# Expert biases as fp32 rows on partitions 96 to 127, and a 22nd early chunk in the long convolution's buffer

## The chip, the core and the metric

The kernel runs on one NeuronCore of a Trainium2 chip. The metric is the device time of one execution in microseconds, as the median of several runs. The profile is one execution recorded by the hardware profiler. Engines are named as in its rows: PE (TensorE matmuls), PEld (its weight loads), DVE (VectorE), ACT (ScalarE), POOL (GpSimd), SP (SyncE, whose queue issues nearly all loads of weights; SPq in the rows).

## What is computed

One step of a one-layer decoder on 264 tokens (256 of a prompt and 8 samples), all in fp32 with a model width of 1024. In short:

```python
proj = rmsnorm(x) @ w_in                      # 7184 columns: q, k, v, z, beta, a, glu, gates
branch_a = gated_delta_net(q, k, v, ...) @ w_gdn_out
branch_b = silu(layernorm(long_conv(glu))) @ w_conf_out     # 31 taps
x = x + (g_a * branch_a + g_b * branch_b) @ w_out
hm = rmsnorm(x)
logits = hm @ w_router + b_router             # top 4 of 32, softmax -> gates
for e in range(32):
    gu = hm @ w_gate_up[e] + b_gate_up[e]     # b_gate_up: 32 rows of 2048
    gate, up = minimum(gu[:, :1024], 7), clip(gu[:, 1024:], -7, 7)
    hid = (up + 1) * gate * sigmoid(1.702 * gate)
    x = x + gates[:, e] * (hid @ w_down[e] + b_down[e])
x = x + (p @ w_ple_proj) * sigmoid(rmsnorm(x) @ w_ple_gate)
y = rmsnorm(x)
```

The outputs are y and the new recurrent and convolution states.

## The kernel before

The weights of the 32 experts are the bulk: each expert has 12 chunks of 128 x 2048 fp32 values (1 MB), 8 of w_gate_up and 4 of w_down. Experts are taken two at a time in 16 groups of 24 chunks; a chunk g of the whole order belongs to group g // 24. In a group the two experts' tokens sit in 64 slots each, and their matmuls run beside each other in the two column halves of the array ([128*64] in the rows).

**Homes.** A chunk lives in a home: one of 12 slots of `ring`, or one of 9 extra buffers (`EXTRA_NAMES`) that earlier stages have left. So `EARLY_CHUNKS` = 21 chunks can be loaded ahead of the expert loop. `home_of` lays the homes out; every chunk from the 21st on goes to the home freed next in order. The homes of chunks 2 and 3 (`ONCE`: gate_up, sig_hid) are used once, as the loop needs them itself. Extra homes are used for chunks below 216 (nine groups), after which the 12 ring slots are left. PE counts `chunk_used`, and SP waits for it before each load in `load_rest_of` (issued by `load_chunk`, L630).

**SP's order before the loop.** SP walks through `stream`: 28 chunks of w_in, 2 of w_conf_out, 4 of w_gdn_out, 4 of w_out (n = 0 to 37) through three ring slots, each waiting for the last use of its slot. `BEFORE` says which early chunks are issued behind step n: at 33 these are chunks 12 and 5. The rest follows by hand (L676 to L704), among it chunk 2 behind waits for `mix` and `bias_ready`.

**Biases.** After the last `mix` ACT loads b_gate_up twice, into rows 0 to 31 and 32 to 63 of `b_stage` in `big` (L1653). ACT casts all 64 rows to fp32r into `bias` (L1660), the first 2048 columns of `lent`. DVE writes into rows 32 to 63 what the cast had lost (L2113, `bias_ready`). So a product of 64 rows with fp32r operands adds high and low part. In each group `selector` (64 x 128, fp32r) says which expert's row goes to which slot, and four products of 512 columns (L1199) open banks 0 to 3, ahead of the chunks' products (L1213). DVE builds the selector (L2152) from `eye2` at first, later from `eye_order`, which follows the order into which the experts are sorted. `lent`'s first columns were the space of the long convolution (`up`, `us`, `conf_sq`) before that, up to `cv_ready`.

**PE at the start of the loop.** After the logits: seven keep_warm products (L1090), the rank matmuls (L1130 to L1135) once DVE has selected, two keep_warm, waits for drained banks; then the gather of group 0 (L1153) after DVE's one-hot, the four bias products, and the chunks. `hm_tok`, from which the gather reads, holds 88 tokens on partitions 0 to 87 of `big`; ACT writes it (L1668) from banks 2 to 7.

**A group in the loop.** Bias products; c = 0 and 1, each followed by four scatter matmuls of the last group (L1283); c = 2 to 7; gather of the next group, transposes; four down steps (L1258). Group 13 does the products of the per-layer embedding as well, and group 15 those of b_down.

Of the kernel before, what the change touches and what calls it, by code (L numbers as in the profile page):

```python
# [43 lines left out]
CAP = 64  # L44
SLOTS = 2 * CAP
# [19 lines left out]
EXTRA_NAMES = ["gate_up", "sig_hid", "rows", "split", "late", "own0", "own1", "pair", "ple"]  # L65
# [101 lines left out]
def _timetable():  # L167
# [29 lines left out]
 gates_in b_high bias_ready e1_ready sp_in ln_ready gT_ready esc_in gcF_ready nsq nrm dec_diff  # L197
# [31 lines left out]
def build(nc, a, out):  # L229
    with ExitStack() as ctx:  # L230
# [10 lines left out]


        def with_split_view(name, cols, split_name, shape):

            t = sbuf(name, [P, cols])
            at = nc.sbuf_base - 4 * cols
            return t, nc.alloc_sbuf_tensor_at(split_name, shape, FP32R, offset=at, align_bytes=32)
# [52 lines left out]
        b_stage = carve(big, (NTB + 1) * D, 2 * D)[0:2 * NE, :]  # L300
# [5 lines left out]
        lent, moe = with_split_view("lent", CONF + CB * T + 24 * (TS * HIST + 11) + KD * T, "moe", [P, 2 * D])  # L306
# [5 lines left out]
        bias = moe[0:2 * NE, 0:2 * D]  # L312
# [36 lines left out]
        eye2 = eye4[0:2 * NE, :]  # L349
        eye_order = sbuf("eye_order", [2 * NE, NE])  # L350
        order = sbuf("order", [1, NE], INT32)
        expert_of = sbuf("expert_of", [TB, 1])
        selector = sbuf("selector", [2 * NE, SLOTS], FP32R)
# [37 lines left out]
        table = small(ROWS, NE)[0:TB]  # L391
        rank, gates = table[:, 0:NTB, :], table[:, NTB:2 * NTB, :]
# [5 lines left out]
        key, top, rest, key_max = small(NE)[0:TB], small(NE)[0:TB], small(NE)[0:TB], small(1)[0:TB]  # L398
        moved, of_top = carve(slots, 0, ROWS, NE)[0:TB], small(ROWS)[0:TB]
# [18 lines left out]
                 "ple": [lent[:, 4 * D:6 * D]]}  # L418
# [159 lines left out]
        def _(sp):  # L578
# [83 lines left out]
            for n, (kind, i) in enumerate(stream):  # L662
# [25 lines left out]
            sp.wait_ge(s["bias_ready"], 1)  # L688
# [55 lines left out]
        def _(pe):  # L744
# [380 lines left out]

            pe.wait_ge(s["consts"], CONSTS + 2)
            b = to_fill(pe, "rank")
            keep_warm(b, 7)
# [58 lines left out]
            def group(sm, sems, prefilled, n, kind, first, last_one, end=False, ple=False):  # L1187
# [6 lines left out]
                pe.wait_ge(sm["selector"], n + 1)  # L1194
# [3 lines left out]
                for t in range(4):  # L1198
                    mm(bank[t][:], selector[:], bias[:, t * 512:(t + 1) * 512], start=True, stop=False)  # L1199
                for c in range(KD):  # L1200
# [20 lines left out]
                    if (end or ple) and c >= 2:  # L1221
                        if c == 2:
                            pe.wait_ge(sm["sc_added"], n * KD)
                            if end:
                                pe.wait_ge(s["bd_loaded"], 16 * 3)
# [79 lines left out]
            pe.wait_ge(s["bias_ready"], 1)  # L1305
            for i in range(2):
                pe.wait_ge(drained[i], before_experts[i])
# [80 lines left out]
        def _(act):  # L1388
# [262 lines left out]
            act.wait_ge(s["mix"], KD)  # L1651
            for i in range(2):
# [125 lines left out]
        def _(dve):  # L1778
# [250 lines left out]

            for kind, n, x in TIMETABLE:  # L2030
# [68 lines left out]
            for i in range(KD):  # L2099
# [43 lines left out]

            def sides(kind, pos):
                at = 0
                for x, cap in kind:
                    yield pos + x, slice(at, at + cap), cap
                    at += cap

            def make_selector(sm, eye, kind, pos):  # L2150
                for at, side, cap in sides(kind, pos):
                    x = v.tensor_copy(selector[:, side], eye[:, bass.ds(at, 1)].broadcast_to([2 * NE, cap]))  # L2152
                x.then_inc(sm["selector"], 1)
# [64 lines left out]
            make_selector(first, eye2, EVEN, 0)  # L2218
            b = to_drain(dve, "rank")
            out_of(v.tensor_copy(count_row, b[0:TB, NTB * NE:(NTB + 1) * NE]), "rank")  # L2220
# [10 lines left out]
            def each_row(x):  # L2231
                return x[:, FREE:].unsqueeze(1).broadcast_to([TB, ROWS, left])

            placed = FULL_AT + SLIM_AT
            for i, pos in enumerate(placed):
# [9 lines left out]
                tell(v.tensor_tensor(moved[:, :, FREE:], table[:, :, pos:pos + 1].broadcast_to([TB, ROWS, left]),  # L2245
# [5 lines left out]
            tell(v.tensor_scalar(eye_order[:], expert_row[0:2 * NE, :], expert_of[0:2 * NE, 0:1], None, ALU.is_equal))  # L2251
# [198 lines left out]
```

## Time and profile before

| | us |
|---|---|
| median of 3 runs | 1419.71 |
| lowest and highest | 1417.78, 1431.76 |
| span of the profiled execution | 1417.1 |
| PE busy in it | 1342.0 (95%) |
| PE weight loads | 749.9 (53%) |
| DVE busy | 477.7 (34%) |
| ACT busy | 291.1 (21%) |
| moved by DMA | 463.23 MB, mean 327 GB/s |

A matmul with fp32 operands is two records (instructions) of the profile, one with fp32r operands is one. A record's duration includes the array's latency, so records that follow one another overlap: the pace is read from the distance of their starts. The profiled execution is 2.6 us under the median of runs. Shares of the whole span mix stages with different limits, so the stages have to be read apart.

### The profile page before, as it was taken

The page shows a single profiled execution, that of the slowest core. Times are in us where ns is not written, and L with a number is a line of the kernel's source. Part 1 is how long each engine was busy: PE and PEld are TensorE (multiplying, and loading weights), DVE is VectorE, ACT ScalarE, POOL GpSimd, SP SyncE. Part 2 cuts the span into 40 slices and gives each one's busy share as a digit, 9 for nine tenths or more (in the row PEclk, how much of TensorE's full clock was granted, in tenths as well). Part 3 has the DMA queues.
Part 4 walks back from the last instruction along what each step waited for, and adds up shares of the span by engine and source line. Part 5 has one row for each costly group of instructions (what it writes and reads, how often), then busy time and mean ns, then how long its engine had stood idle before and what let it go on. Part 6 is the DMA issues. An engine that isn't in the chain of part 4 may idle for free.

```text
span 1417.1 us, 21577 instructions
## 1 busy us (share of the span) xinstructions
PE 1342.0 (95%) x8363; PEld 749.9 (53%) x8363; DVE 477.7 (34%) x1203; ACT 291.1 (21%) x673; POOL 26.6 (2%) x64
## 2 busy tenths in 40 slices
PE   8999999999999999999999898898989899999996
PEld 7877777768885444434434434344333434534355
DVE  3666868763235221122122211212212022121224
ACT  4645453525012100000001000001000000101024
POOL 3000000000000000000000000000000000000000
PEclk9999989999999999999999999999999999999998
DMA  7325243453767999999999999999999999999971
GB/s 220 139 91 154 92 123 151 153 209 122 294 230 277 405 421 420 421 420 421 421 420 419 421 421 421 421 421 422 421 420 421 420 421 416 420 421 421 420 292 32
DMA packets 86524, 463.23 MB, mean 327 GB/s; under 512 B 11141, under 2 KB 29086, under 8 KB 33326
## 3 DMA queue, kind: packets, MB, share of 16 engines
q1 hardware_dynamic: 70229, 452.99, 78.9%
q10 hardware_dynamic: 16193, 8.84, 2.2%
q8 instruction: 69, 1.13, 0.3%
q14 instruction: 33, 0.27, 0.0%
HBM read 455.78 MB, written 6.68 MB: 326 GB/s over the span
## 4 chain that ended last, share of the span: by engine, by line
PE 62%; DMA 21%; SPq 6%; DVE 5%; ACT 3%; issue 2%; ACTq 0%; POOL 0%; DVEq 0%; POOLq 0%
PE bank L1213 18%; DMA ring<-in_w_gate_up 16%; PE bank L1258 11%; PE bank L1021 10%; SPq L630 6%; PE bank L1153 5%; DMA ring<-in_w_down 4%; PE bank L1068 3%; PE bank L1283 2%; PE bank L1102 2%; PE bank L1326 2%; DMA dedicated<-in_w_gate_up 2%; DVE lent L2025 1%; PE bank L1267 1%; PE bank L849 1%
## 5 line engine op out<-in xcount | busy, mean ns | idle before, releaser
L1213 PE MATMUL bank<-ring,lent 128*64 128x512 f32 (+1 forms) x1832 | 385.7, 598 | 34.7 <-DMA ring<-in_w_gate_up 34.2
L1213 PEld LDWEIGHTS bank<-ring,lent 128*64 128x64 f32 (+1 forms) x1832 | 120.1, 131 | 249.5 <-issue 247.8
L1021 PE MATMUL bank<-lent,ring 128*128 128x264 f32 x896 | 231.3, 400 | 5.1 <-ACT lent L1613 1.6
L1258 PE MATMUL bank<-ring,lent 128*64 128x512 f32 (+1 forms) x928 | 182.7, 594 | 3.0 <-DMA ring<-in_w_down 3.0
L1021 PEld LDWEIGHTS bank<-lent,ring 128*128 128x128 f32 x896 | 163.1, 192 | 41.1 <-issue 10.2
L1698 ACT ACTIVATE big<-big 128x256 f32<-128x256 f32 x64 | 26.7, 417 | 509.2 <-DVE big L2196 509.2
L2196 DVE TENSOR_SCALAR big<-bank 128x256 f32<-128x256 f32 x64 | 27.0, 423 | 268.8 <-PE bank L1213 268.8
L1258 PEld LDWEIGHTS bank<-ring,lent 128*64 128x64 f32 (+1 forms) x928 | 58.0, 129 | 112.3 <-issue 111.0
L1153 PE MATMUL bank<-st,big 88*128 88x128 f32 x768 | 88.9, 275 | 0.6 <-ACT pair_space L1704 0.5
L1153 PEld LDWEIGHTS bank<-st,big 88*128 88x128 f32 x768 | 87.2, 192 | 3.0 <-issue 1.6
L2215 DVE TENSOR_TENSOR xT<-xT,bank 128x264 f32<-128x264 f32 x128 | 54.9, 429 | 96.6 <-PE bank L1283 78.1
L2152 DVE CAST selector<-eye_order 64x64 fp32r (+3 forms) x30 | 4.6, 185 | 242.9 <-PE bank L1213 242.9
L1689 ACT COPY outputs<-bank 128x512 f32<-128x512 f32 x32 | 17.2, 589 | 221.7 <-PE bank L1258 221.7
L1283 PE MATMUL bank<-rstd,outputs 128*128 128x264 f32 x240 | 61.4, 399 | 0.0
L2025 DVE SCALAR_TENSOR_TENSOR lent<-lent,spare 128x256 f32<-128x256 f32 x120 | 58.2, 485 | 4.3
L1283 PEld LDWEIGHTS bank<-rstd,outputs 128*128 128x128 f32 x240 | 43.1, 189 | 30.3 <-issue 24.4
L1267 PEld LDWEIGHTS bank<-ident,big 128*128 128x128 f32 x128 | 20.4, 205 | 36.3 <-issue 32.8
L1213 PE MATMUL bank<-dedicated,lent 128*64 128x512 f32 (+1 forms) x120 | 36.3, 596 | 0.0
L2199 DVE TENSOR_TENSOR big<-big 128x256 f32<-128x256 f32 x64 | 27.2, 426 | 22.7 <-ACT big L1698 19.3
L1267 PE MATMUL bank<-ident,big 128*128 128x128 f32 x128 | 30.0, 317 | 2.8 <-DVE big L2200 2.8
L1683 ACT COPY lent<-bank 128x512 f32<-128x512 f32 x32 | 18.7, 587 | 66.8 <-PE bank L1153 66.8
L1102 PE MATMUL bank<-lent,ring 128*128 128x264 f32 x128 | 29.7, 387 | 1.1 <-DVE lent L2095 1.1
(438 smaller groups left out, 1397.8 us busy)
## 6 DMA issues: line engine op xcount, KB each, us to landing
ring<-in_w_gate_up SPq DMA_DIRECT2D x205, 1024.0 KB, 23.5
ring<-in_w_down SPq DMA_DIRECT2D x100, 1024.0 KB, 24.1
ring<-in_w_in SPq DMA_DIRECT2D x28, 1024.0 KB, 5.0
dedicated<-in_w_gate_up SPq DMA_DIRECT2D x13, 1024.0 KB, 23.8
dedicated<-in_w_down SPq DMA_DIRECT2D x9, 1024.0 KB, 24.1
late<-in_w_gate_up SPq DMA_DIRECT2D x8, 1024.0 KB, 22.9
outputs<-in_w_gate_up SPq DMA_DIRECT2D x7, 1024.0 KB, 24.9
lent<-in_w_gate_up SPq DMA_DIRECT2D x7, 1024.0 KB, 22.3
```

The costliest lines, as they stand in the source:

```text
L630: sp.dma_start(dst, src).then_inc(sem, 16)
L1021: last = mm(b[:, 0:T], w[:, k, o:o + P], aT[:, k, :], start=k == 0, stop=k == KD - 1)
L1068: last = mm(b[:, 0:T], w[:, k, o:o + P], rhs(k), start=k == 0, stop=k == n_k - 1)
L1102: last = mm(b[:, 0:T], w[:, k, o:o + P], aT[:, k, :], start=k == 0, stop=k == KD - 1)
L1153: last = mm(aux[h][:, i * SLOTS:(i + 1) * SLOTS], hm_tok[0:TB, j, k * P:(k + 1) * P], onehot[:, j, :], start=j == 0, stop=j == NTB - 1)
L1213: last = mm(bank[q][lo:hi, :], x_slots[:, 4 * half + k, lo:hi], w, start=False, stop=half == 1 and k == 3)
L1258: last = mm(bank[4 + t][lo:hi, :], hT[:, m, lo:hi], w, start=m == 0, stop=m == KD - 1)
L1267: last = tr(bank[q][:, k * P:(k + 1) * P], rows_of[:, k, :], ident[:])
L1283: mm(bank[SCATTER_BANKS[i]][:, 0:T], y[:, i * P:(i + 1) * P], spread, start=True, stop=True).then_inc(sm["sc_filled"], 1)
L1326: last = mm(b[:, 0:T], w[:, k, P * (i % 2):P * (i % 2) + P], aT[:, k, :], start=k == 0, stop=k == KD - 1)
L2025: tell(v.scalar_tensor_tensor(x, up[:, i, tap:tap + TP], w, x, ALU.mult, ALU.add))
L2215: v.tensor_tensor(xT[:, i, :], xT[:, i, :], bank[banks[i]][:, 0:T], ALU.add).then_inc(sm["sc_added"], 1)
```

## The change

It does two things.

*Biases.* `bias` becomes 32 plain fp32 rows on partitions 96 to 127 of `big`, columns 0 to 2047, beside the rows of `hm_tok`. One load fills it, issued by ACT after `onorm_ready` 5. The second load, ACT's cast and DVE's subtraction are gone, and SP's wait for `bias_ready` with them. `selector`, `eye_order`, `expert_of` and the sorted `table` get their rows on partitions 96 to 127, the products have 32 rows and fp32 operands. In front of group 0 the products for banks 2 and 3 stand in the place of five keep_warm, that for bank 0 in the place of the two keep_warm after the rank matmuls; only that for bank 1 stays between the gather and c = 0. In all later groups four stand where four stood. The first selector is made by DVE during the out-projection.

*Early chunk.* The first 2048 columns of `lent` become an extra home "conv": 22 early chunks. Chunk 21 is issued behind chunks 12 and 5 at step 33, after a wait for `cv_ready`.

```diff
-EXTRA_NAMES = ["gate_up", "sig_hid", "rows", "split", "late", "own0", "own1", "pair", "ple"]
+EXTRA_NAMES = ["gate_up", "sig_hid", "rows", "split", "late", "own0", "own1", "pair", "ple", "conv"]
-BEFORE = {20: [17], 21: [18], 25: [13, 4], 26: [7, 8], 32: [0, 1], 33: [12, 5], 34: [6, 19]}
+BEFORE = {20: [17], 21: [18], 25: [13, 4], 26: [7, 8], 32: [0, 1], 33: [12, 5, 21], 34: [6, 19]}
+AFTER_CONF = 33
...
-        b_stage = carve(big, (NTB + 1) * D, 2 * D)[0:2 * NE, :]
+        bias = carve(big, 0, 2 * D)[BIAS_ROWS]
...
-        bias = moe[0:2 * NE, 0:2 * D]
...
-        selector = sbuf("selector", [2 * NE, SLOTS], FP32R)
+        selector = sbuf("selector", [P, SLOTS])
...
-                 "ple": [lent[:, 4 * D:6 * D]]}
+                 "ple": [lent[:, 4 * D:6 * D]], "conv": [lent[:, 0:2 * D]]}
...
+                if n == AFTER_CONF:
+                    sp.wait_ge(s["cv_ready"], 1)
                 for i in BEFORE.get(n, []):
                     load_first(i)
...
             sp.wait_ge(s["mix"], KD)
-            sp.wait_ge(s["bias_ready"], 1)
             load_first(2)
...
+            def bias_products(t):
+                mm(bank[t][:], selector[BIAS_ROWS, :], bias[:, t * 512:(t + 1) * 512], start=True, stop=False)
...
-            keep_warm(b, 7)
+            keep_warm(b, 2)
+            pe.wait_ge(s["bd_loaded"], 16)
+            pe.wait_ge(first["selector"], 1)
+            for t in (2, 3):
+                pe.wait_ge(drained[t], before_experts[t])
+                bias_products(t)
             pe.wait_ge(s["selected"], 1)
...
-            for i in range(2, 8):
+            pe.wait_ge(drained[0], before_experts[0])
+            bias_products(0)
+            for i in range(4, 8):
                 pe.wait_ge(drained[i], before_experts[i])
-            keep_warm(bank[2], 2)
...
-                for t in range(4):
-                    mm(bank[t][:], selector[:], bias[:, t * 512:(t + 1) * 512], start=True, stop=False)
+                for t in (1,) if opening else range(4):
+                    bias_products(t)
...
-            act.wait_ge(s["mix"], KD)
-            for i in range(2):
-                act.dma_start(b_stage[NE * i:NE * (i + 1), :], a["b_gate_up"][0]).then_inc(s["bd_loaded"], 16)
+            act.wait_ge(s["onorm_ready"], 5)
+            act.dma_start(bias, a["b_gate_up"][0]).then_inc(s["bd_loaded"], 16)
...
-                if k == 1:
-                    act.wait_ge(s["bd_loaded"], 16 * 2)
-                    nc.scalar.copy(bias, b_stage).then_inc(s["b_high"], 1)
...
-                    dve.wait_ge(s["b_high"], 1)
-                    low_rows = slice(NE, 2 * NE)
-                    tell(v.tensor_tensor(bias[low_rows], b_stage[low_rows], bias[low_rows].bitcast(FP32), ALU.subtract),
-                         "bias_ready")
+                    make_selector(first, eye4, EVEN, 0)
```

## Rows read from the trace of the kernel before

**Rows 1.** The page's slices: transfer rate in 40 equal parts of the span.

```profile
GB/s 220 139 91 154 92 123 151 153 209 122 294 230 277 405 421 420 421 420 421 421 420 419 421 421 421 421 421 422 421 420 421 420 421 416 420 421 421 420 292 32
```

**Rows 2.** Windows: length, busy time (instructions) of each engine, clock, DMA share, GB/s.

```profile
510.00:770.00 260.00, 260.00 (x1501) 111.31 (x1497) 53.34 (x141) 24.43 (x59) 0.00 (x0) 1.00 1.01 420
860.00:1000.00 140.00, 128.90 (x653) 59.32 (x655) 26.61 (x71) 12.06 (x29) 0.00 (x0) 1.00 1.01 421
```

**Rows 3.** Waits, whole span: who waited for whom, total us, times, longest.

```profile
PE bank L1213 <- DMA ring<-in_w_gate_up: 34.2, 35, 2.5
```

**Rows 4.** PE in order of time, groups 1 and 6: start us, us, what.

```profile
494.17 1.20 PE L1199 MATMUL bank<-moe,selector 64*128 64x512 f32 x4
...
765.68 1.20 PE L1199 MATMUL bank<-moe,selector 64*128 64x512 f32 x4
```

**Rows 5.** Windows in group 0.

```profile
450.00:451.00 1.00, 1.00 (x8) 0.38 (x6) 0.89 (x4) 0.00 (x0) 0.00 (x0) 1.00 0.00 0
484.00:486.00 2.00, 2.00 (x12) 0.66 (x10) 0.00 (x0) 0.00 (x0) 0.00 (x0) 1.00 0.84 236
```

**Rows 6.** PE in order of time, groups 13, 14 and 15 and the last chunk.

```profile
1188.70 1.20 PE L1199 MATMUL bank<-moe,selector 64*128 64x512 f32 x4
...
1252.13 1.20 PE L1199 MATMUL bank<-moe,selector 64*128 64x512 f32 x4
...
1309.74 1.20 PE L1199 MATMUL bank<-moe,selector 64*128 64x512 f32 x4
...
1365.46 3.65 PE L1258 MATMUL bank<-ring,lent 128*64 128x512 f32 x16 [1.31 <-DMA ring<-in_w_down]
```

**Rows 7.** SP's queue in order of time, 372 to 443 us.

```profile
372.96 0.90 SPq L630 DMA_DIRECT2D ring<-in_w_gate_up  x2
...
379.71 0.33 SPq L667 DMA_DIRECT2D ring<-in_w_out  x1
...
442.50 10.97 SPq L630 DMA_DIRECT2D ring<-in_w_down  x3
```

**Rows 8.** Windows around the start of the out-projection.

```profile
370.00:392.00 22.00, 22.00 (x101) 18.78 (x100) 5.18 (x13) 0.00 (x0) 0.00 (x0) 1.00 1.00 405
392.00:394.00 2.00, 1.92 (x9) 1.31 (x7) 0.00 (x0) 0.00 (x0) 0.00 (x0) 1.00 0.42 176
394.00:396.00 2.00, 1.02 (x5) 0.90 (x6) 0.93 (x3) 0.00 (x0) 0.00 (x0) 1.00 0.51 147
```

**Rows 9.** PE in order of time, out-projection to group 0.

```profile
394.98 7.39 PE L1102 MATMUL bank<-lent,ring 128*128 128x264 f32 x32 [1.06 <-DVE lent L2095]
...
429.14 3.36 PE L1090 MATMUL bank<-pT,ones 128*128 128x264 f32 x14
432.33 0.27 PE L1130 MATMUL bank<-st 88*88 88x32 f32 x2
...
434.82 2.94 PE L1153 MATMUL bank<-st,big 88*128 88x128 f32 x24
437.70 1.20 PE L1199 MATMUL bank<-moe,selector 64*128 64x512 f32 x4
438.82 3.65 PE L1213 MATMUL bank<-ring,lent 128*64 128x512 f32 x16
```

**Rows 10.** Line L1199: duration ns min/median/max, first and last start.

```profile
L1199 PE MATMUL bank<-moe,selector x64: 388/394/497, 437.7 to 1310.6; 64*128 64x512 f32 x64
```

**Rows 11.** PE in order of time at 102 us: products of four rows.

```profile
102.05 1.13 PE L1006 MATMUL bank<-late,spare 4*128 4x512 f32 x4
```

**Rows 12.** ACT in order of time, 429 to 439 us.

```profile
429.17 4.26 ACT L1668 ACTIVATE big<-bank,st 88x512 f32<-88x512 f32 x6 [0.36 <-DVE st L2118]
...
437.86 0.59 ACT L1683 COPY lent<-bank 128x512 f32<-128x512 f32 x1 [2.09 <-PE bank L1153]
```

**Rows 13.** DVE in order of time, out-projection.

```profile
411.65 2.28 DVE L2113 TENSOR_TENSOR moe<-big,moe 32x2048 fp32r<-32x2048 f32 x1
```

**Rows 14.** Waits of SP's queue, 480 to 490 us.

```profile
SPq L630 <- PE bank L1258: 15.1, 2, 12.4
```

More of the change, by code:

```diff
@@ L44 @@
 CAP = 64
+BIAS_ROWS = slice(96, 128)
 SLOTS = 2 * CAP
@@ L305, in build @@
         CONF = CB * 286 + CB * 248
-        lent, moe = with_split_view("lent", CONF + CB * T + 24 * (TS * HIST + 11) + KD * T, "moe", [P, 2 * D])
+        lent = sbuf("lent", [P, CONF + CB * T + 24 * (TS * HIST + 11) + KD * T])
         conf = carve(lent, 0, CONF)
@@ L390, in build @@
         ROWS = 2 * NTB + 2
-        table = small(ROWS, NE)[0:TB]
-        rank, gates = table[:, 0:NTB, :], table[:, NTB:2 * NTB, :]
+        table = small(ROWS, NE)
+        rank, gates = table[0:TB, 0:NTB, :], table[0:TB, NTB:2 * NTB, :]
         expert_row, count_row = table[:, 2 * NTB, :], table[:, 2 * NTB + 1, :]
@@ L397, in build @@
         root_t, rstd_t = small(NTB)[0:TB], small(NTB)[0:TB]
[L398 to L399 removed]
+        key, top, rest, key_max = small(NE), small(NE), small(NE), small(1)
+        moved, of_top = carve(slots, 0, ROWS, NE), small(ROWS)
         before = small(TB)[0:TB]
@@ L1193, in group @@
                     pe.wait_ge(sm["x_ready"], n * 2 + 2)
-                pe.wait_ge(sm["selector"], n + 1)
+                    pe.wait_ge(sm["selector"], n + 1)
                 if not first:
@@ L1304, in _ @@
             gather(first, 0, (0,))
-            pe.wait_ge(s["bias_ready"], 1)
-            for i in range(2):
-                pe.wait_ge(drained[i], before_experts[i])
+            pe.wait_ge(drained[1], before_experts[1])
             group(first, loaded, None, 0, EVEN, True, False)
@@ L2028, in over_blocks, with sides, make_selector @@
                 return x.unsqueeze(1).broadcast_to([P, CB, T])
+            def sides(kind, pos):
+                at = 0
+                for x, cap in kind:
+                    yield pos + x, slice(at, at + cap), cap
+                    at += cap
+            def make_selector(sm, eye, kind, pos):
+                for at, side, cap in sides(kind, pos):
+                    x = v.tensor_copy(selector[BIAS_ROWS, side], eye[BIAS_ROWS, bass.ds(at, 1)].broadcast_to([NE, cap]))
+                x.then_inc(sm["selector"], 1)
             for kind, n, x in TIMETABLE:
@@ L2142, in quarter @@
                 return x[:, QUARTER_COLS * q:QUARTER_COLS * (q + 1)]
[L2144 to L2153, printed above, removed]
             def make_onehot(sm, n, kind, pos, low=0):
@@ L2217, in _ @@
             make_onehot(first, 0, EVEN, 0)
-            make_selector(first, eye2, EVEN, 0)
             b = to_drain(dve, "rank")
-            out_of(v.tensor_copy(count_row, b[0:TB, NTB * NE:(NTB + 1) * NE]), "rank")
+            out_of(v.tensor_copy(count_row, b[:, NTB * NE:(NTB + 1) * NE]), "rank")
             dve.wait_ge(s["wexp"], NTB)
@@ L2231, in each_row @@
             def each_row(x):
-                return x[:, FREE:].unsqueeze(1).broadcast_to([TB, ROWS, left])
+                return x[:, FREE:].unsqueeze(1).broadcast_to([P, ROWS, left])
             placed = FULL_AT + SLIM_AT
@@ L2244, in _ @@
                 tell(v.tensor_reduce(of_top[:], moved[:, :, FREE:], AX.X, ALU.add))
-                tell(v.tensor_tensor(moved[:, :, FREE:], table[:, :, pos:pos + 1].broadcast_to([TB, ROWS, left]),
+                tell(v.tensor_tensor(moved[:, :, FREE:], table[:, :, pos:pos + 1].broadcast_to([P, ROWS, left]),
                                      each_row(top), ALU.mult))
@@ L2250, in _ @@
             tell(v.tensor_copy(order[:], expert_row[0:1, :]), "order_ready")
-            tell(v.tensor_scalar(eye_order[:], expert_row[0:2 * NE, :], expert_of[0:2 * NE, 0:1], None, ALU.is_equal))
+            tell(v.tensor_scalar(eye_order[BIAS_ROWS], expert_row[BIAS_ROWS], expert_of[BIAS_ROWS, 0:1], None, ALU.is_equal))
             tell(v.tensor_copy(key[:], count_row))
@@ L2389, in _ @@
                 pool.wait_ge(s[f"state_stored{j}"], 16 * 4)
-            tell(g_.iota(iota_int[:, 0:NE], pattern=[[1, NE]], base=0, channel_multiplier=0))
-            tell(g_.tensor_copy(expert_row, iota_int[:, 0:NE]))
+            numbers = order_int[:]
+            tell(g_.iota(numbers, pattern=[[1, NE]], base=0, channel_multiplier=0))
+            tell(g_.tensor_copy(expert_row, numbers))
             tell(g_.iota(iota_int, pattern=[[1, NO_RANKS + CAP]], base=int(FAR), channel_multiplier=0))
             tell(g_.tensor_copy(iota, iota_int))
-            for i in range(2):
-                r = slice(NE * i, NE * (i + 1))
-                tell(g_.iota(iota_int[r, 0:1], pattern=[[0, 1]], base=0, channel_multiplier=1))
-                tell(g_.tensor_copy(expert_of[r, :], iota_int[r, 0:1]), "consts" if i else None)
+            tell(g_.iota(numbers[BIAS_ROWS, 0:1], pattern=[[0, 1]], base=0, channel_multiplier=1))
+            tell(g_.tensor_copy(expert_of[BIAS_ROWS, :], numbers[BIAS_ROWS, 0:1]), "consts")
             tell(g_.affine_select(out=before, in_=ones[0:TB, 0:TB], compare_op=ALU.is_ge, fill=0.0, base=-1,
```

17 lines of the change are left out of this document (6 added, 11 removed).

## The prediction

> **What bounds the kernel now.** I read the page's slices first, then busy time in windows, then the waits, then the order of instructions at the places the diff touches.
>
> The slices show two halves [rows 1]. Up to the twelfth slice (about 425 us) the transfers are irregular. From the fourteenth to the thirty-eighth they run at 405 to 422 GB/s without a break, while PE is at nine tenths too. The windows tell which of the two sets the pace: between 510 and 770 us PE is busy 260.00 of 260 us; between 860 and 1000 us only 128.90 of 140, at the same 420 and 421 GB/s [rows 2]. So in the first part of the expert loop PE works off the early chunks and is its own bound. From about 770 us it has eaten its stock and waits for every pair of chunks. What the waits name there is the expert weights: 34.2 us in 35 waits [rows 3].
>
> The price of a group for PE: the bias products of group 1 begin at 494.17, those of group 6 at 765.68, so five groups take 271.5 us, 54.3 each [rows 4]. The price of a group for DMA: 24 chunks of 1,048,576 bytes at 421 GB/s, 2.49 us each, 59.8 us. DMA is the slower by 5.5 us per group. It is never short of work after 456 us but for a dip to 236 GB/s at 484 to 486 [rows 5]. Hence the end of the expert loop is the moment at which DMA's unbroken stream started, plus the number of chunks left at that moment times 2.49 us; after the last landing come some 52 us which this change doesn't touch (the last chunk's products begin at 1365.46 [rows 6]). Two things can shorten the run: fewer chunks in the stream, or an earlier start of it. PE work inside the loop costs nothing as long as PE still ends before the data.
>
> **The change part by part.**
>
> *The 22nd early chunk.* Chunk 21 (the first of the stream now) is issued in the n=33 step, behind chunks 12 and 5, whose issue is at 372.96 [rows 7]. Its new wait, for cv_ready, is over before: PE waits for cv_ready ahead of the conv-out products, and this SP step has already waited for a later product (ba1). Nothing is queued behind it longer than now. The transfer itself takes 2.49 us of DMA time. DMA is full until 392 us and then not: 176 and 147 GB/s in 392 to 396 [rows 8], which is 2.5 us of idle time in those four. The w_out chunks behind it on the queue land up to 2.5 us later. The first is issued at 379.71 [rows 7], with three chunks' worth ahead of it, so it lands some 8 to 10 us later, and is needed at 394.98 [rows 9]; each further one is needed two column blocks (7.5 us) after the last: hidden. If the cover were gone, PE would start the out-projection late by at most 2.5 us. The two 256 KB loads of b_gate_up behind the last mix become one, and move ahead of this stretch, so it is lighter by 1.2 us as well.
>
> In the stream, every later chunk goes one place further back in the rotation, so nothing else moves. The first two homes freed (chunks 0 and 1) come at 442.50 as now, then come no more for 10.97 us on SP [rows 7], because homes 2 and 3 are used once; DMA stands still at 450 to 451 [rows 5]. That hole stays. The stream has 362 chunks of experts where it had 363: **-2.49 us**.
>
> At this point the Trainium skill ("DMA: Bandwidth & Descriptors", Specifications) gives an HBM limit per core of about 358 GB/s. By it a chunk would be worth 2.9 us, an estimate from that page. The trace disagrees: 421 GB/s over 140 us [rows 2], and the sum goes by the row.
>
> *Start of the stream.* Its first free home comes when PE has finished c=0 of group 0. Before: gather from 434.82, four fp32r bias products from 437.70, c=0 from 438.82 [rows 9]. The four took 1.12 us, 0.28 each. After: only the product for bank 1 stands there, in fp32. An fp32 matmul is two records of 2 cycles a column: keep_warm's 14 records of 264 columns fill 429.14 to 432.33, 0.228 each [rows 9], so 512 columns take 0.44, and the pair some 0.86 to 0.88. The fp32r product has one record of 388 to 497 ns [rows 10]. The nearest fp32 shape with few rows gives bounds: four records of 4x512, in two row groups, in 1.13 us [rows 11]. If they ran one after the other, a record is 0.28 and a product 0.56; if two at a time, 0.56 and 1.13. I take 0.86, since columns and passes set the 264-column records, which lie in between: c=0 can begin at 438.56. It also needs x_ready, ACT's copy from 437.86 for 0.59, over at 438.45 [rows 12], no limit. Gain **0.26 us** (bounds: 0 at 1.13 us, 0.3 at 0.56, where x_ready holds it).
>
> The other three: products for banks 2 and 3 take the place of five of seven keep_warm matmuls. 429.14 plus two warm ones is 430.05. Bank 3 must be drained by the second of ACT's six copies from 429.17, 4.26 us for six [rows 12], at 430.6, so both products are done by 431.8, before the selection at 432.3. The product for bank 0 (0.86) replaces two keep_warm (0.88) after the rank matmuls; the gather behind it waits for DVE's one-hot until 434.8 anyway. Nothing gained, nothing lost; PE's idle gap of half a microsecond ahead of 432.3 has no cost at a granted clock that is full throughout. If bank 3 were drained late, up to 0.5 us would be lost.
>
> *Removed on DVE and ACT.* DVE's subtraction, 2.28 us at 411.65 [rows 13], and ACT's cast ahead of it stand beside the out-projection, in which PE is continuously busy: 0. DVE's selector copies (0.29 us) move from the stretch after the one-hot to this one; the count copy behind them isn't waited for by the gather: 0. SP no longer waits for bias_ready, whose end is this subtraction, and issues chunk 2 some 3 us sooner; its next step waits for an out-projection product as before: 0. On POOL a few constants go, long before their use: 0. The sorting of experts on 128 instead of 88 partitions keeps its columns: 0.
>
> *fp32 bias products in the loop.* In each of 15 groups four products at 0.86 to 0.90 stand where four took 1.12: +2.3 to 2.5 us of PE per group, 34 to 37 us in all. This is the large number of the change, and it must be shown to be hidden. Group 15 starts at 1309.74 [rows 6]. PE's own work would have let it start at 494.17 + 14 x 54.30 + 9.1 (group 13 with its per-layer products takes 63.4, 1188.70 to 1252.13 [rows 6]) = 1263.5. So PE has 46.2 us to spare, 43.5 against a stream that ends 2.75 earlier. After the change 6 to 9 us are left. PE then meets the data at about group 10 or 11 instead of 6. Locally: group 13 costs PE 65.8 against 62.3 for DMA (25 chunks with w_ple), 3.5 behind; group 14 costs 56.7 against 59.8; group 15 catches up the rest, before its down part. Cost **0**. If the cover were gone, each further 0.1 us per product would cost 6 us.
>
> The other side of this: PE frees homes later, so DMA could be starved. The dip at 484 to 486 follows 12.4 us in which SP waits for a home [rows 14]. The next gap, from the end of group 0 to c=0 of group 1, grows from 4.7 to 7.0 us; but in the ten microseconds ahead of it PE frees 8 chunks and DMA moves 4, so 10 us of work stand in the queue. From group 9 on the chunks rotate over 12 homes only. With PE about 5 chunks behind, 7 are open, 17 us, against gaps of at most 9.5 us without a freed home. Not starved.
>
> *Row groups.* If a product on rows 96 to 127 could run beside its neighbours, the loop's cost would be smaller, and hidden all the same. All four share those rows and the neighbours use all 128, so I expect none of it.
>
> Sum: -2.49 - 0.26 = -2.75 us. The profiled execution's span of 1417.1 becomes 1414.3. The median of runs is 1419.7, 2.6 above the span; so **1417.0**.
>
> **Rivals.**
> 1. *PE takes over as the bound* (slower). One mechanism: bias products in the loop cost more than 0.86. Price: 60 products; the point from which it decides is 0.28 + 43.5/60 = 1.0 us each. For it: such a shape, 32 rows on partition 96 under fp32, isn't in the trace, its bound reaches 1.13, and the margin is only 6 to 9 us. Against: the two-records pattern of the full-height fp32 matmuls. At 1.13 us each it would be 51 - 43.5 = 7.5 over the data: 1424.5. Chance 0.08.
> 2. *The early chunk brings nothing*: it pushes the w_out chunks so that PE starts the out-projection 2.5 us late, which delays the stream by what it saves. For it: DMA moves 400 GB/s from 370 to 392 [rows 8]. Against: at least 5 us of slack for each chunk. Time 1419.5. Chance 0.1.
> 3. *More is gained*: the dip at 484 closes, or PE's gap ahead of the rank matmuls turns out to gain. About 1 us more: 1416. Chance 0.1.
>
> **How the numbers follow.** The forecast (-2.75, with bounds -3.3 to -2.0, that is 1416.4 to 1417.7, from the start's gain of 0 to 0.3 and half a microsecond either way) has 0.72. Three runs of before spread from 1417.8 to 1431.8 about 1419.7, so a median moves by 2 us of itself. Range 1413 to 1421.5: it takes in rivals 2 and 3 and that spread, and leaves out rival 1. One per cent (14 us) is about what a measurement of this kernel can tell from no change. None of the cases reaches it; rival 1 would need 1.25 us per product. Faster by over 1%: 0.02, within: 0.94, slower: 0.04.
>
> **What would show it.** In the new trace: 22 early chunks, with L630 issuing a lent chunk near 374; c=0 of group 0 at about 438.5; the four bias products at 3.4 to 3.5 us from group 1 on, a period of 56.6 to 56.8 us until PE first waits, at about 1050 to 1150 instead of 770; 420 GB/s throughout; the last chunk's products at about 1362.7. Wrong would be: gaps in the transfers after 500, the last landing not followed by its products at once, or bias products above 1 us.

## The result and the profile after

The changed kernel takes 1439.62 us (median of six runs, 1431.58 to 1443.55) against 1420.57 before. The ratio is 1.0133, 95% interval 1.0111 to 1.0155: 19 us (1.3%) slower, where I had forecast 2.7 us less. The profiled execution's span is 1438.1.

The slices of its page, the clock that was granted to TensorE and the transfer rate, answer [rows 1]:

```profile
PEclk9999989999998999999999999999999999999998
GB/s 217 136 90 152 91 149 121 149 206 134 353 217 240 380 421 421 419 421 421 421 420 419 421 420 420 421 363 358 421 420 421 421 421 414 421 419 421 421 242 32
```

The transfers, unbroken in the kernel before, drop to 363 and 358 GB/s in the middle. The mean granted clock is 0.969 against 0.993. Windows in the manner of [rows 2] (length, busy time and instructions by engine, then clock, DMA share, GB/s):

```profile
510.00:770.00 260.00, 260.00 (x1320) 107.50 (x1323) 55.33 (x146) 21.62 (x53) 0.00 (x0) 0.97 1.01 420
860.00:1000.00 140.00, 140.00 (x648) 58.16 (x646) 30.30 (x80) 11.02 (x27) 0.00 (x0) 0.96 0.96 390
```

PE is busy 140.00 of 140 us where it had waits before, at a clock of 0.96. In the whole expert loop no wait of PE for a weight chunk is left (the wait of [rows 3] is gone). PE has become the bound, and its granted clock falls again and again. Where it falls is seen in PE's instructions in order of time, group 1 and group 3, with the end of the loop; they answer [rows 4] and [rows 6]:

```profile
502.59 3.70 PE L1122 MATMUL bank<-big,selector 32*128 32x512 f32 x8
506.22 3.65 PE L1217 MATMUL bank<-ring,lent 128*64 128x512 f32 x16
...
617.87 4.49 PE L1122 MATMUL bank<-big,selector 32*128 32x512 f32 x8
622.29 6.21 PE L1217 MATMUL bank<-ring,lent 128*64 128x512 f32 x16
...
1331.72 3.69 PE L1122 MATMUL bank<-big,selector 32*128 32x512 f32 x8
...
1390.83 1.35 PE L1297 MATMUL bank<-rstd,outputs 128*128 128x264 f32 x5 [0.80 <-ACT outputs L1687]
```

L1122 are the bias products, L1217 of 16 records the products of c = 0 (the first chunk pair of a group). In group 1 they take 3.63 and 3.6 us. In group 3 the products take 4.4 us and c = 0 takes 6.2: 3.35 us more together, so for about 6.7 us TensorE worked at half its clock, 1.2 instead of 2.4 GHz. Such a fall begins in 12 of the 15 groups (2 to 13), at the bias products or within half a microsecond behind them; it costs 1.4 to 1.7 us in nine of them and 3.35 in three. The traces of bias_alone and four_32rows below have it in the same twelve. Why groups 1, 14 and 15 have none, no run settles.

The opening, answering [rows 9]:

```profile
428.69 1.14 PE L1085 MATMUL bank<-pT,ones 128*128 128x264 f32 x4
429.75 1.98 PE L1122 MATMUL bank<-big,selector 32*128 32x512 f32 x4
...
433.46 2.07 PE L1122 MATMUL bank<-big,selector 32*128 32x512 f32 x2
435.46 5.49 PE L1157 MATMUL bank<-st,big 88*128 88x128 f32 x24
440.88 2.07 PE L1122 MATMUL bank<-big,selector 32*128 32x512 f32 x2
442.88 5.46 PE L1217 MATMUL bank<-ring,lent 128*64 128x512 f32 x16
448.27 2.94 PE L1157 MATMUL bank<-st,big 88*128 88x128 f32 x24
```

The single product for bank 0 takes 2.0 us where it would take 0.9, the gather 5.4 instead of 2.9, c = 0 5.4 instead of 3.6. c = 0 is over at 448.3; before it was 442.4. A second fall follows in group 0, from 484 to 491, at its first down products, which took 0.64 us a record before:

```profile
486.54 1.12 PE L1262 MATMUL bank<-late,lent 128*64 128x512 f32 x1
```

**The sum closes.** Group 1 begins 8.4 us later (502.59 against 494.17): 5.9 are lost up to the end of c = 0, most of the rest in that second fall. Fifteen groups carry 2.51 us more of bias products (3.63 instead of 1.12), 37.7. The falls are 24.7 together (the group periods less 56.8, and less 9.1 more in group 13). That is 70.8 us of PE time. PE had 49.5 us to spare up to the last scatter (46.2 at group 15's start and 3.3 of waits in it). 21.3 are left over; the last scatter stands at 1390.83 against 1369.89, 20.9 later.

### The profile page after: what moved, and what is told of

It is laid out like the page before. It is cut to its first block, busy times and chain, and to the rows that moved or that the text cites. A ratio compares the mean times of both kernels' runs of the same rounds, so it can differ in the third digit from the quotient of the medians.

```text
span 1438.1 us, 21668 instructions
## 1 busy us (share of the span) xinstructions
PE 1404.5 (98%) x8413; PEld 759.7 (53%) x8413; DVE 475.7 (33%) x1202; ACT 289.1 (20%) x672; POOL 26.4 (2%) x62
## 4 chain that ended last, share of the span: by engine, by line
PE 90%; DVE 5%; ACT 3%; issue 2%; ACTq 0%; POOL 0%; DVEq 0%; POOLq 0%
PE bank L1217 33%; PE bank L1262 16%; PE bank L1016 10%; PE bank L1157 6%; PE bank L1122 4%; PE bank L1287 4%; PE bank L1063 3%; PE bank L1097 2%; PE bank L1328 2%; PE bank L1271 2%; DVE lent L2023 1%; PE bank L844 1%; PE bank L1188 1%; DVE outputs L1986 0%; DVE spare L1986 0%
## 5 line engine op out<-in xcount | busy, mean ns | idle before, releaser
L1217 PE MATMUL bank<-ring,lent 128*64 128x512 f32 (+1 forms) x1808 | 375.3, 621 | 0.0
L1016 PE MATMUL bank<-lent,ring 128*128 128x264 f32 x896 | 231.3, 400 | 5.1 <-ACT lent L1615 1.6
L1217 PEld LDWEIGHTS bank<-ring,lent 128*64 128x64 f32 (+1 forms) x1808 | 110.6, 135 | 233.0 <-issue 230.4
L1016 PEld LDWEIGHTS bank<-lent,ring 128*128 128x128 f32 x896 | 163.1, 192 | 41.0 <-issue 10.2
L1262 PE MATMUL bank<-ring,lent 128*64 128x512 f32 (+1 forms) x896 | 178.4, 593 | 0.0
L1262 PEld LDWEIGHTS bank<-ring,lent 128*64 128x64 f32 (+1 forms) x896 | 56.8, 132 | 111.6 <-issue 110.4
L2036 DVE COPY selector<-eye_order 32x64 f32 (+3 forms) x30 | 4.7, 190 | 297.2 <-PE bank L1217 297.1
L1122 PE MATMUL bank<-big,selector 32*128 32x512 f32 x128 | 65.1, 646 | 0.0
L1217 PE MATMUL bank<-dedicated,lent 128*64 128x512 f32 x112 | 51.4, 612 | 0.0
L1122 PEld LDWEIGHTS bank<-big,selector 32*128 32x128 f32 x128 | 22.8, 189 | 35.3 <-issue 35.0
```

Of the source, the lines that this page charges most:

```text
L1016: last = mm(b[:, 0:T], w[:, k, o:o + P], aT[:, k, :], start=k == 0, stop=k == KD - 1)
L1122: mm(bank[t][:], selector[BIAS_ROWS, :], bias[:, t * 512:(t + 1) * 512], start=True, stop=False)
L1217: last = mm(bank[q][lo:hi, :], x_slots[:, 4 * half + k, lo:hi], w, start=False, stop=half == 1 and k == 3)
L1262: last = mm(bank[4 + t][lo:hi, :], hT[:, m, lo:hi], w, start=m == 0, stop=m == KD - 1)
```

## The experiments

All times are in us. The ratios are against runs of the kernel before on the same chip, whose median was 1420.57 for the changed kernel and 1419.5 to 1419.8 for the others.

| run | rows, and where the products stand in the loop | median | ratio, 95% interval |
|---|---|---|---|
| changed kernel | 32, four together | 1439.62 | 1.0133 (1.0111 to 1.0155) |
| bias_alone | the same, no 22nd chunk | 1438.97 | 1.0132 (1.0115 to 1.0149) |
| four_32rows | 32, four together | 1434.78 | 1.0103 (1.0086 to 1.0120) |
| four_128rows | 128, four together | 1421.19 | 1.0008 (0.9998 to 1.0018) |
| spread_32rows | 32, one by one | 1422.33 | 1.0017 (1.0007 to 1.0027) |
| pairs_32rows | 32, two by two | 1421.53 | 1.0013 (1.0004 to 1.0023) |
| before_fp32_64rows | 64, four together | 1422.24 | 1.0020 (1.0011 to 1.0030) |
| before_fp32r_32rows | 32, one record each | 1420.11 | 1.0005 (0.9995 to 1.0014) |
| before_loop_work | before, 2.6 us more per group | 1421.21 | 1.0008 (0.9999 to 1.0017) |
| before_late_group0 | before, 2.6 us more in group 0 | 1423.60 | 1.0025 (1.0014 to 1.0036) |
| bias_once | bias in group 0 alone | 1420.27 | 1.0009 (0.9998 to 1.0020) |
| bias_once_no_conv | the same, no 22nd chunk | 1422.62 | 1.0022 (1.0012 to 1.0032) |
| mixed_rows | 32 in the opening, 128 after | 1425.46 | 1.0047 (1.0034 to 1.0061) |
| mixed_2 | 32 only ahead of the selection | 1417.92 | 1.0003 (0.9988 to 1.0017) |
| mixed_3 | one product of 32 rows | 1418.77 | 0.9997 (0.9987 to 1.0007) |

### Do the 32 rows lower the clock?

`four_32rows` puts the changed kernel's opening back into the order of the kernel before, and keeps all else:

```diff
-            keep_warm(b, 2)
-            ... bias_products(2), bias_products(3)
+            keep_warm(b, 7)
...
-            bias_products(0)
+            keep_warm(bank[2], 2)
...
-                for t in (1,) if opening else range(4):
+                for t in range(4):
                     bias_products(t)
```

> The changed kernel with the opening's order as in the kernel before: seven and two keep_warm products, then all four bias products (fp32, 32 rows) between the gather and c = 0. It is the base for the next run, which differs only in the rows. Theory (a stretch of about 3.5 us in which only 32 of 128 rows work lets TensorE's clock fall, and PE becomes the bound): the granted clock falls at the bias products in most groups, and the time stays near the changed kernel's, 1434 to 1444 us. Rival (PE is the bound only because fp32 products take more columns' time, the clock fell for another reason, such as power under a busier PE): the same time, 1434 to 1444, but the falls are not tied to the bias products. Rival 2 (the lost time is in the opening's new order, 5.9 us there and what follows from it): about 6 to 8 us less than the changed kernel, 1432.

It came out at 1434.78 in the median of four runs, not far from rival 2's 1432. But its profiled execution took 1439.6, as the changed kernel's did, has falls in the same twelve groups, and begins group 1 at 502.16, since the four products in the opening now bring a fall there too. Its other runs are 4 to 6 us quicker, at a mean clock of 0.975 to 0.976; what they do in the opening can't be seen. So the opening's new order is at most a small part of the 19 us.

`four_128rows` is that kernel with other rows:

```diff
-                mm(bank[t][:], selector[BIAS_ROWS, :], bias[:, t * 512:(t + 1) * 512], start=True, stop=False)
+                mm(bank[t][:], selector[:], big[:, t * 512:(t + 1) * 512], start=True, stop=False)
...
+                    tell(v.memset(selector[0:96, :], 0.0))
                     make_selector(first, eye4, EVEN, 0)
```

> As four_32rows, but each bias product is taken over all 128 rows: the selector's rows 0 to 95 are zero, so the sum is the same, as is the number of columns and passes. Theory (few rows at work let the clock fall): no fall of the clock, bias products 3.4 to 3.6 us per group as in four_32rows, group period 56.7 us, the stream of chunks is the bound again; 1417.1 - 2.5 for the chunk + 2.3 for the three more products ahead of c = 0, so a span of 1417 and a median of 1419.5, 15 to 20 us less than four_32rows. Rival (the length of the fp32 products alone makes PE the bound, or a busier PE lets the clock fall whatever the rows): the same as four_32rows, 1434 to 1444. If zeros do not count as work for whatever lowers the clock, this run looks like four_32rows too.

The bias products' records (ns min/median/max) in four_32rows, then in four_128rows:

```profile
L1122 PE MATMUL bank<-big,selector x128: 587/587/1052, 437.2 to 1334.5; 32*128 32x512 f32 x128
```

```profile
L1122 PE MATMUL bank<-big,selector x128: 591/592/697, 436.2 to 1314.5; 128*128 128x512 f32 x128
```

Same columns, passes and sums. With 128 rows no record is over 697 ns, where the lower clock gave up to 1052, none of the 16 groups has a fall at its bias products, and 13.6 us are gone. So what lowers the clock here is that a stretch of these products keeps only 32 of the array's rows at work; rows of zeros do count. The theory stands, and the rival of a busier PE falls. The Trainium skill ("TensorE: Matmul & The Clock Gate", Part 1) says that the clock gate is set by how busy the PE has lately been, and lists two states of it, 1.2 and 2.4 GHz. The trace agrees on the two: a window that lies wholly in a fall shows 0.50, one outside 1.00. By the page's words PE was busy here all the time and nothing should have fallen; the rows show that the height of the products counts.

`spread_32rows` moves each product ahead of its own bank's first chunk product; `pairs_32rows` (the same with `c % 4 == 0` and two products) makes stretches twice as long:

```diff
-                for t in (1,) if opening else range(4):
-                    bias_products(t)
                 for c in range(KD):
+                    if c % 2 == 0:
+                        bias_products(c // 2)
...
-                    make_selector(sm, eye_order, after, pos + 2)      # behind the first chunk used
...
+                if not last_one:                                      # at the end of the group
+                    make_selector(sm, eye_order, after, pos + 2)
```

> The changed kernel with the bias products of 32 rows apart: each stands right ahead of the first chunk product of its own bank (c = 0, 2, 4, 6), in all groups and in the opening, where the keep_warm products are as in the kernel before. DVE makes the next selector at the end of its group. Same products, same columns, same rows. Theory (it takes a stretch of low work, not a sum of it): no fall of the clock, period 56.7 us, the stream is the bound, and the start is the one I forecast for the change: span 1414.3, median 1417. Rival (32-row fp32 products lower the clock however they lie, or their time alone makes PE the bound): 1430 to 1444.

> As spread_32rows, but two products together ahead of c = 0 and two ahead of c = 4: stretches of 1.8 us with 32 rows, where spread_32rows has 0.9 and four_32rows 3.6. Theory (the length of the stretch counts): fewer falls than four_32rows (12 of 16 groups there) or none; 1421 to 1424 without any, up to 1432 if some groups fall. Rival (any stretch of more than one product falls as the four do): 1434 and more.

Their records, in this order:

```profile
L1122 PE MATMUL bank<-big,selector x128: 587/640/692, 437.2 to 1346.7; 32*128 32x512 f32 x128
```

```profile
L1122 PE MATMUL bank<-big,selector x128: 587/587/692, 436.6 to 1336.2; 32*128 32x512 f32 x128
```

No record of theirs is over 692 ns: no fall at 0.9 us, and none at 1.8. One fall in the loop of pairs_32rows, at 1131.8, comes after two products and a wait for a chunk of 1.9 us; the kernel before has one at the same place, at 1129.7, also after a wait, with nothing of 32 rows near:

```profile
1129.74 5.32 PE L1213 MATMUL bank<-ring,lent 128*64 128x512 f32 x16 [2.45 <-DMA ring<-in_w_gate_up]
```

So the same 3.6 us of 32-row work cost nothing of the clock once full rows stand between. (The "12 of 16 groups" in the text above leave out group 0: four_32rows has falls in 13 of 16.) The expected gain of the chunk was missed, though: 1422.33 in spread_32rows instead of 1417. A product apart costs 1.05 us instead of 0.91, and something else was late; this led to the question of the stream below.

`before_fp32_64rows` changes one line of the kernel before, `before_fp32r_32rows` another:

```diff
-mm(bank[t][:], selector[:], bias[:, t * 512:(t + 1) * 512], start=True, stop=False)
+mm(bank[t][:], selector[:].bitcast(FP32), bias[:, t * 512:(t + 1) * 512].bitcast(FP32), start=True, stop=False)
```

```diff
-mm(bank[t][:], selector[:], bias[:, t * 512:(t + 1) * 512], start=True, stop=False)
+mm(bank[t][:], selector[0:NE, :], bias[0:NE, t * 512:(t + 1) * 512], start=True, stop=False)
```

> The kernel before, with the operands of its 64-row bias products read as fp32 instead of fp32r: same rows, same values, two records a product instead of one, 3.6 us a group where four took 1.12. No early chunk. Theory (a stretch of 3.6 us with few rows at work lets the clock fall; with 128 rows it did not): I do not know on which side 64 rows lie. If half the rows are enough, no fall, and only the 2.5 us ahead of c = 0 of group 0 count, with what they cost in the opening: 1422 to 1424. If half are too few, falls in most groups as with 32 rows, and 1434 to 1444. Rival (zeros and rows do not matter, the partitions or the buffer that the changed kernel reads do): no fall here, 1422 to 1424.

> The kernel before, with bias products of the high part alone: 32 rows, fp32r, one record a product, 1.12 us a group. It leaves out the low part of the gate_up bias. Theory (few rows lower the clock only when they last for the greater part of some microseconds): no fall, the time of the kernel before, 1418 to 1421. Rival (any product of 32 rows between full ones costs clock, however short): falls, over 1425.

Their records:

```profile
L1199 PE MATMUL bank<-moe,selector x128: 589/589/693, 437.5 to 1318.7; 64*128 64x512 f32 x128
```

```profile
L1199 PE MATMUL bank<-moe,selector x64: 386/392/500, 437.2 to 1311.7; 32*128 32x512 f32 x64
```

64 rows for 3.6 us: no fall at the products. 32 rows for 1.1 us: none. The 2.5 us that the former is slower fit the 2.5 us of PE work ahead of c = 0 in group 0; no run separates them. So in the loop it took both, few rows and four fp32 products in a row. One rival of before_fp32_64rows is left: all falls were seen with rows on partitions 96 to 127, and four fp32 products of 32 rows elsewhere were not tried. With 128 rows, which take in those partitions, nothing fell, so it could only be that place with no other rows at work.

### Is the added PE time hidden, and is the chunk worth 2.5 us?

> The kernel before with six full-height keep_warm products (2.6 us of PE, about what the fp32 bias products add) at the start of groups 1 to 15 and nothing else. Theory (the added PE time in the loop is nearly hidden as long as the clock stays up): 1 us more or less, 1419 to 1421.5. Rival (PE time of this size makes PE the bound by itself, and the clock's fall is a side show): over 1430.

It adds `keep_warm(aux[0], 6)` at the start of groups 1 to 15 of the kernel before. By its trace that is 2.9 us per group (a period of 57.2 against 54.3), a little more than the change adds. It is 1.4 us slower in the median, and the interval holds no change (its upper end is 2.4 us). My step "cost 0" for 34 to 37 us of PE work is right to within about that, as long as the clock stays up.

> The changed kernel without the 22nd early chunk (21 as before; chunk 21 is loaded in the stream). Theory (PE is the bound in the changed kernel from the opening to the end): the early chunk is worth nothing there, so the time is the changed kernel's within 1 us, 1437 to 1442. Rival (the transfers still set the end, as I had forecast): 2.5 us more, 1442.

1438.97 against 1439.62, and 1438.0 against 1438.1 in the profiled executions: in the changed kernel the chunk is worth nothing that can be seen, because PE sets the end.

`bias_once` is spread_32rows in which groups 1 to 15 have no bias products, so it leaves their gate_up bias out; the first chunk product of each bank has start=True. Its twin lacks the 22nd chunk.

> spread_32rows with bias products in group 0 alone; in groups 1 to 15 the first chunk product of each bank opens the bank and the gate_up bias is left out. So PE has 1.1 us less per group than in the kernel before, and the 22nd early chunk is there. Theory (chunk by chunk, the early chunk takes 2.49 us off the stream where the stream sets the end): 2.5 us less than bias_once_no_conv, and, with the start of c = 0 at 438.2, a span near 1414 to 1416 and a median near 1417 to 1418. Rival (the chunk brings nothing, since it delays something at the start or the stream's rate pays for it): equal times.

> bias_once without the 22nd early chunk (21 as in the kernel before). Theory: the stream sets the end as in the kernel before, 1419 to 1421, which is 2.5 us over bias_once. Rival: equal to bias_once.

1420.27 (1418.0 to 1421.8) against 1422.62 (1421.3 to 1423.4): 2.35 us, where I had said 2.49. The price of an early chunk is right. But both were slower than I had expected, with less PE work than the kernel before. So the start of the stream was misjudged:

> The kernel before with six full-height keep_warm products (2.6 us of PE) ahead of c = 7 in group 0 alone. Theory (the transfers run dry between the last gate_up chunk and the first down chunk of group 0, at 484 to 486, so that whatever delays the down part there delays the stream and the end): 2.6 us more, 1422 to 1423. Rival (my forecast: the stream starts with c = 0 of group 0, and PE work behind that is hidden): no change, 1419.7.

3.8 us slower (2.0 to 5.1 by the interval), from 2.6 us of PE work that my forecast would have hidden. Four windows of it, which answer [rows 5]:

```profile
484.00:486.00 2.00, 2.00 (x8) 0.68 (x6) 0.75 (x3) 0.00 (x0) 0.00 (x0) 0.50 0.18 64
486.00:488.00 2.00, 2.00 (x8) 0.52 (x6) 0.00 (x0) 0.00 (x0) 0.00 (x0) 0.74 0.00 0
488.00:490.00 2.00, 2.00 (x12) 0.70 (x10) 0.00 (x0) 0.00 (x0) 0.00 (x0) 1.00 0.34 57
490.00:492.00 2.00, 2.00 (x12) 0.62 (x10) 0.00 (x0) 0.00 (x0) 0.00 (x0) 1.00 0.76 307
```

DMA all but stands still from about 485 to 490. In the kernel before that was a dip worth 0.9 us (236 instead of 421 GB/s for two), which I had read and passed over: it says that the queue runs dry just there. It gets its next work when the first down chunks of group 0 are used. That issue in SP's queue, here in the kernel before, before_late_group0 and bias_once_no_conv:

```profile
483.96 0.33 SPq L630 DMA_DIRECT2D late<-in_w_gate_up  x1
```

```profile
488.70 0.33 SPq L630 DMA_DIRECT2D late<-in_w_gate_up  x1
```

```profile
489.16 0.33 SPq L624 DMA_DIRECT2D late<-in_w_gate_up  x1
```

The last scatters, in the same order, and behind them that of bias_once, whose issue is at 488.55:

```profile
1369.89 3.80 PE L1293 MATMUL bank<-rstd,outputs 128*128 128x264 f32 x16 [0.77 <-ACT outputs L1689]
1374.12 3.80 PE L1295 MATMUL bank<-rstd,outputs 128*128 128x264 f32 x16 [0.77 <-ACT outputs L1691]
1374.17 3.80 PE L1292 MATMUL bank<-rstd,outputs 128*128 128x264 f32 x16 [0.77 <-ACT outputs L1685]
1371.58 3.80 PE L1292 MATMUL bank<-rstd,outputs 128*128 128x264 f32 x16 [0.77 <-ACT outputs L1685]
```

That is 885.9, 885.4 and 885.0 us after the issues with 21 early chunks, and 883.0 with 22. So the end is fixed by the down part of group 0, not by its c = 0.

Of the 4.7 us by which before_late_group0 issues later, 2.8 stand ahead of the down part, 2.6 of them the added products. The rest is a fall of the clock to 0.50 (first two windows). It follows a stretch of 4.6 us in which PE waits twice for DVE's hidden rows (the input of the down products) and does only short transposes and small matmuls. The kernel before has the same stretch:

```profile
477.85 0.51 PE L1267 MATMUL bank<-ident,big 128*128 128x128 f32 x2 [1.53 <-DVE big L2200]
479.62 0.50 PE L1267 MATMUL bank<-ident,big 128*128 128x128 f32 x2 [1.27 <-DVE big L2200]
```

Its profiled execution has no fall there. It is the exception: each of the other 15 traces, of whatever kernel, has one of 3.4 or 6.8 us that begins between 478 and 485. So this fall isn't the work of the 32 rows, and the trace from which I forecast was quick by it. Why that one execution was spared isn't settled.

### The opening

> A version meant to be the best: the changed kernel, with the products of 32 rows in the opening kept apart (a keep_warm product between those for banks 2 and 3), and the products in groups 1 to 15 over 128 rows (the selector's other rows zero). Theory (the clock falls for a long stretch of few rows only; transfers run dry in group 0, so the time at which its down part begins sets the stream): no fall at bias products, down part of group 0 no later than 484.5, the chunk's 2.4 us gained, and in the last three groups PE about 1 us behind the data: span 1415 to 1417, median 1417 to 1419. Rival (no fall needs full rows also for the short products in the opening): the opening late by some us as in the changed kernel, 1422 and more.

> mixed_rows with the opening's products for banks 0 and 1 (behind the rank matmuls, and between the gather and c = 0) over 128 rows; those for banks 2 and 3, ahead of the selection, stay at 32 rows with a keep_warm product between. Theory A (the 32-row products next to the small rank matmuls and the gather let the clock fall): no fall, c = 0 at 438.3, median 1417 to 1418.5. Theory B (those ahead of the selection, in the place of five keep_warm, do it): a fall as in mixed_rows, 1424 to 1426.

> As mixed_2, but only one product of 32 rows (bank 2) ahead of the selection, with three keep_warm before and two behind; that for bank 3 stands with that for bank 1 between the gather and c = 0, over 128 rows, 0.9 us later. Theory A: no fall, 0.9 us over mixed_2. Theory B: no fall here if one such product is few enough, 1418 to 1419.5, and then 5 us or more under mixed_2.

The edits: mixed_rows is the changed kernel with `keep_warm(b, 1)` between the products for banks 2 and 3, and with all-row products (as in four_128rows) in groups 1 to 15. mixed_2 takes the all-row form for banks 0 and 1 of the opening too. mixed_3 has `keep_warm(b, 3)`, bank 2, `keep_warm(b, 2)` ahead of the selection, and bank 3 with bank 1.

PE in order of time, gather, last bias product, c = 0, in mixed_rows and in mixed_2:

```profile
434.94 4.71 PE L1162 MATMUL bank<-st,big 88*128 88x128 f32 x24
439.58 2.07 PE L1122 MATMUL bank<-big,selector 32*128 32x512 f32 x2
441.58 5.83 PE L1225 MATMUL bank<-ring,lent 128*64 128x512 f32 x16
```

```profile
434.26 2.94 PE L1162 MATMUL bank<-st,big 88*128 88x128 f32 x24
437.05 1.02 PE L1125 MATMUL bank<-big,selector 128*128 128x512 f32 x2
438.00 3.65 PE L1225 MATMUL bank<-ring,lent 128*64 128x512 f32 x16
```

mixed_rows missed its 1417 to 1419 by over 6 us; its rival came true. It has no fall at the products of groups 1 to 15, but its opening has one of 10.2 us from 435.8. Apart or not, the 32-row products around the small rank matmuls let the clock fall in the opening; with all rows for two of them it stayed up in the profiled execution, as theory A had it. mixed_2 and mixed_3 are the quickest medians of the study, 1417.92 and 1418.77, each with an interval that holds no change: no version is shown to be faster than the kernel before. mixed_2's runs lie in two groups, six at 1416.2 to 1418.0 with a mean granted clock of 0.993 to 0.995, and four at 1420.9 to 1423.6 with 0.988 to 0.991. So the clock was low for longer in the slow ones, and mixed_2 isn't free of falls. With two such groups neither its median, below that of the kernel before, nor its ratio, above 1, tells much. Where it fell in them can't be seen, as only one execution has a profile.

## Why the prediction was wrong

- **The bound.** Right for the kernel before, and right that 34 to 37 us of PE work fit behind the transfers (before_loop_work, four_128rows). The failing step is in "fp32 bias products in the loop": its "Cost **0**" took each group at the duration of products at full clock, and in the opening I wrote that PE's gap has no cost "at a granted clock that is full throughout". That was a reading of the old work, carried over to new work of another shape, and not even quite true of the old (0.50 for 3.4 us at 1129.7). The four products of 32 rows in a row took the clock away: 24.7 us in the loop, where I had 0, besides the 5.9 us that the single ones cost in the opening. By the sum above the PE time then exceeds what was to spare by 21.3 us; with 128 rows in their place it does not (four_128rows).
- **The term's size.** A product takes 0.91 us, not 0.86: 3 us over 60 products. With them the margin of 6 to 9 us is 3 to 6. It is a small error beside the first, but four_128rows shows the margin used up: from group 13 on, PE no longer waits for a chunk.
- **The rival.** "PE takes over as the bound" is what happened, but not by its mechanism (over 1.0 us for a product of unusual shape). Each product at full clock was below that point. My 0.08 had weighed only the duration, so neither the range nor the chance of slower (0.04) had the clock in it. A slip beside it: one per cent more would have needed 1.29 us per product, not 1.25, since the gain of 2.75 us had to be used up first.
- **Start of the stream.** Wrong twice. The gain of 0.26 us was a loss of 5.9 at the end of c = 0, by the clock (a fall of 13.7 us from 432.9). And the anchor was the wrong one: DMA runs dry at 484, so group 0's down part sets the stream. I had used the dip to show that DMA is *nearly* never idle; it was the sign that the queue had no reserve there. The 2.6 us between span and median that I added were not all noise either: in every run the time is 1.7 to 1.9 us over its own span.
- **The early chunk.** Right: 2.35 us measured for 2.49, with nothing delayed at the out-projection (PE starts it at 394.53 in the changed kernel; the chunk is issued at 373.46). It is not seen in the result because the end had moved to PE.
- **The removed casts and waits.** 0, as said: the out-projection's products run without a gap in both traces.

## What to carry to other kernels

Cost a new matmul by its duration, and then ask how much of the array it uses and what stands around it: here a stretch of low products halved the clock for itself and for the full ones behind it. If such products are needed, give them more rows, even zeros: the product took the same time (592 ns a record against 587), and the clock stayed up. Full-height products between them did as well in the loop, but not in the opening. And read a short dip in a saturated queue as the place where it may have no reserve: here 2.6 us of work put ahead of that place delayed the end by 3.8.

## What the runs showed of the hardware

Four fp32 products of 32 rows in a row (3.6 us) came with half clock in 12 of 15 groups (2 to 13) in three traces, while PE was not idle there. Four of 64 or of 128 rows never did (before_fp32_64rows, four_128rows), nor did one or two of 32 rows between full-height work in the loop (spread_32rows, pairs_32rows), but for one place in the latter that is behind a wait of PE. In the opening of mixed_rows, beside matmuls of 32 and 64 columns, single ones were enough; in that of spread_32rows a single one right ahead of c = 0 was not. Zero rows count like others. A fall shows itself in records of up to 1052 ns where 587 is usual. In the loop it lasted 3.4 us, at a cost of 1.4 to 1.7 us, or twice that.
